# Two modulation groups moved from the delta stage into the ring of weight slabs and the norm chains

## The chip, the core and the metric

The kernel runs on one core of a Trainium2 chip. The metric is the device time of one execution in microseconds. Engines are named as in the profile: PE is TensorE, DVE VectorE, ACT ScalarE, POOL GpSimd, and SP is the engine whose queue issues most of the transfers.

## The reference, cut to what matters

A two-layer encoder step works on 256 prompt tokens and 64 decode tokens, D = 1024. Layer 0 is a gated delta-rule mixer with a dense SwiGLU, layer 1 is forgetting attention with an eight-expert mixture. Each sub-layer is scaled, shifted and gated by vectors made from a condition `c`:

```python
mod = (sc @ p['ada_w'][l] + p['ada_b'][l])[:, None, :]
sh_m, sc_m, gt_m, sh_f, sc_f, gt_f = jnp.split(mod, 6, axis=-1)
h = _rmsnorm(x, p['pre_mix_g'][l]) * (1 + sc_m) + sh_m
...
x = x + gt_m * _rmsnorm(y, p['post_mix_g'][l])
...
kvm = (sc @ p['kv_ada_w'] + p['kv_ada_b'])[:, None, :]
sh_kv, sc_kv = jnp.split(kvm, 2, axis=-1)
```

`sc` is silu(c) for the two streams, so these products have two rows, while their weights are 2 x 24 MB and 8 MB in float32: 56 slabs of 1 MB.

## The kernel before

**Modulation.** The 56 slabs form seven groups of eight: groups 0 to 2 are layer 0, group 3 the shared key/value modulation, groups 4 to 6 layer 1. `ada_load` puts slab n into a ring of six places of its own. `ada_pe` is called with a count of units: a unit is either the four products of one slab (L323, which add into bank 0), or, as the ninth unit of a group, the turn (L330). Before the turn ACT copies the bank to `ada_rows` (L339), and after it DVE adds the bias into `mod` (L350). Group 0 is done in the setup stage; groups 1 to 6 are done in `unit_phase` and `delta_phase`, from calls of `ada_pe`, `ada_act` and `ada_dve` written between the stage's own steps by hand. The calls of the three engines have to name the same units in the same order.

**Delta stage.** The loop over `steps` has 15 steps, five levels for each of three items (two of 8 heads, one of 4). A step is `update(j)` (L1346, L1349), one unit, `product(j + 2)` (L1332), one more unit. DVE masks each product (L1586) and ACT copies each update back (L1716, L1721). After the loop come `off` (L1356), `join` (L1364), the state products (L1369 and others) with further units between them, then a norm, whose output feeds `w_out`. The scratch of this stage lies in the memory of the weight ring, so that `w_out` slabs load only from its end on.

**Weight ring.** All other weights pass as slabs of 1 MB through `raw`, six places. `load(n)` waits on SP until slab n - 6 is split (`raw_split`), then issues one transfer, or two of half a slab for `ffn_up`. ACT and DVE split a slab into a high and a low part (L268, L275) two slabs ahead of PE (`AHEAD`), and `dense_tiles` does the products, three for each pair of parts (L354 to L356).

**Mixed phase.** `mixed_phase` runs twice here: `w_out` (4 slabs), and `ffn_down` (12 slabs). Its last part is the norm chain: PE sums squares over the partitions (L768, L770, then L772, L774), ACT makes the inverse root, DVE adds the residual and forms the next norm (L862 to L866), and ACT ends it (L816, L817). On SP the phase issues the loads six slabs ahead; the first of the two then also stores the last rows of the convolution, and waits for those stores:

```python
for n in range(n0, n0 + n_slabs):
    k.load(sp, n + RAW)
if row_out is not None:
    sp.wait_ge(sig["copied"].sem, copied0 + QKV_T // 4)
    for q in range(QKV_T // 4):
        ...
        k.store(sp, 0, k.o["conv"][s][0, 0][:, 512 * q:512 * q + 512], row_out[rows, q // 4, :])
    sp.wait_ge(k.stores[0], k.n_store[0])
```

**Blocks.** Each phase is one `nc.Block()` with a program for each engine. At its end all engines wait for each other; in the trace these are the rows "PEq L735" and the like.

After the first mixed phase comes `ffn_up_phase` (22 slabs), after the second `copy_phase` with `kv_w` (4 slabs). Both begin with the rest of the norm (`Renewal.act`, `Renewal.dve`), and their tiles wait for it.

Of the kernel before, what the change touches and what calls it, by code (L numbers as in the profile page):

```python
# [54 lines left out]
ADA_GROUP = 8  # L55

# [108 lines left out]
def ada_slabs(i):  # L165

    def wide(w, c0, c1):
        w = w.rearrange("(k p) n -> p k n", p=P)
        return [w[:, k0:k0 + KT // 2, c:c + 512] for c in range(c0, c1, 512) for k0 in (0, KT // 2)]
    ada = i["ada_w"]  # L170
    return wide(ada[0], 0, 6 * D) + wide(i["kv_ada_w"], 0, 2 * D) + wide(ada[1], 0, 6 * D)


class Kernel:


    def __init__(self, nc, ctx, i, o):
# [4 lines left out]
        self.ada_src = ada_slabs(i)  # L182
        sb = self.sb
# [33 lines left out]
        self.junk = self.x_flat[:, KT * T + T:KT * T + T + 1]  # L217
# [27 lines left out]
    def load(self, sp, n):  # L245

        if n >= len(self.slabs):
            return
        if n >= RAW:
            sp.wait_ge(self.raw_split, n - RAW + 1)  # L250
        for words, cols, kts, src in self.slabs[n]:
            width = sum(part[1] for part in self.slabs[n])
            sp.dma_start(self.slab_view(self.raw, n % RAW, words, cols, kts, width), src).then_inc(self.raw_full[n % RAW], 16)

    def full_count(self, n):

        return 16 * sum(len(self.slabs[m]) for m in range(n % RAW, n + 1, RAW))
# [4 lines left out]
    def split_hi(self, act, n):  # L262

        words = self.used(n)
        act.wait_ge(self.raw_full[n % RAW], self.full_count(n))
        if n >= SPL:
            act.wait_ge(self.split_read, n - SPL + 1)
        act.activation(self.w_hi[:, n % SPL, 0:words], self.raw[:, n % RAW, 0:words], ACT.Copy).then_inc(self.hi_ready, 1)  # L268

    def split_lo(self, dve, n):  # L270

        words = self.used(n)
        dve.wait_ge(self.raw_full[n % RAW], self.full_count(n))
        dve.wait_ge(self.hi_ready, n + 1)
        dve.tensor_tensor(self.w_lo[:, n % SPL, 0:words], self.raw[:, n % RAW, 0:words],  # L275
                          self.w_hi[:, n % SPL, 0:words], ALU.subtract).then_inc(self.raw_split, 1)
# [14 lines left out]
    def ada_load(self, sp, n):  # L291
# [3 lines left out]
        sp.dma_start(self.ada_ring[n % (2 * SPL)], self.ada_src[n]).then_inc(self.ada_full[n % (2 * SPL)], 16)  # L295

# [16 lines left out]
    def ada_pe(self, pe, count=1):  # L313


        for g, j, n in self.ada_unit("pe", count):
            if j < ADA_GROUP:
                pe.wait_ge(self.ada_full[n % (2 * SPL)], 16 * (n // (2 * SPL) + 1))
# [3 lines left out]
                for q in range(KT // 2):  # L322
                    last = pe.matmul(self.ps[0][32 * q:32 * q + 32, :],  # L323
                                     self.c_pad[:, half * (KT // 2) + q, C_AT - 2 * block:C_AT - 2 * block + 32],
                                     self.ada_ring[n % (2 * SPL)][:, q, :], start=(j == 0), stop=(j == ADA_GROUP - 1))
                last.then_inc(self.ada_read, 1)
            else:
                pe.wait_ge(self.ada_copied, g + 1)
                for q in range(4):
                    last = pe.matmul(self.ps[0][:, 8 * q:8 * q + 8], self.ada_rows[:, q * P:(q + 1) * P], self.ada_sum[:],  # L330
# [3 lines left out]
    def ada_act(self, act, count=1):  # L334

        for g, j, n in self.ada_unit("act", count):
            if j == ADA_GROUP:
                act.wait_ge(self.ada_read, n)
                act.activation(self.ada_rows[:], self.ps[0][:], ACT.Copy).then_inc(self.ada_copied, 1)  # L339

    def ada_dve(self, dve, count=1):

        for g, j, n in self.ada_unit("dve", count):
            if j == ADA_GROUP:
                dve.wait_ge(self.ada_turned, g + 1)
                tiles = slice(16 * g, 16 * g + 16)
                mod = self.mod[:, tiles, :].rearrange("p (j q) s -> p q j s", q=4)
                bias = self.vec_a[:, tiles].rearrange("p (j q) -> p q j", q=4).unsqueeze(3).to_broadcast([P, 4, 4, 2])
                got = self.ps[0][:, 0:32].rearrange("p (q j s) -> p q j s", q=4, j=4)
# [31 lines left out]
def setup_phase(k):  # L381
# [3 lines left out]
    with nc.sbuf_tensor("row_squares", [P, D], F32) as row_squares, \  # L385
# [59 lines left out]
        def _(sp):  # L445
            for n in range(ADA_GROUP - 1):
                k.ada_load(sp, n)
            k.load(sp, 0)
            k.ada_load(sp, ADA_GROUP - 1)
            for n in range(1, 3):  # L450
                k.load(sp, n)
# [268 lines left out]
def mixed_phase(k, n0, n_slabs, n_k, x_hi, x_lo, gate, gain, sums, renewal, row_out=None):  # L720
# [14 lines left out]
    with nc.Block() as block:  # L735
# [20 lines left out]
        def _(pe):  # L756
# [8 lines left out]

            dense_tiles(k, pe, n0, n_slabs, n_k, x_hi, x_lo, k.ps[0:6], bank_free, half_done=sig["part"].sem, last_slab=old_sums)
            pe.wait_ge(sig["summed"].sem, summed0 + KT - 2)
# [136 lines left out]

def conv_phase(k, h32, h_hi, h_lo, qkv, z_silu, last_rows, lnb, g):
# [6 lines left out]
    with nc.sbuf_tensor("xp", [P, 4, T + 6], F32) as xp, nc.sbuf_tensor("conv_acc", [P, 2, T + 3], F32) as acc, \  # L912
# [11 lines left out]
        def _(sp):  # L924
            for n in range(n0 + 3, n0 + n_slabs):
# [3 lines left out]
                k.load(sp, n)  # L929
# [187 lines left out]
def delta_phase(k, qkv, lnb, g, oT, z_silu, hi, lo, last_rows):  # L1117
# [19 lines left out]
    with ExitStack() as mem:  # L1137
# [101 lines left out]
        def _(sp):  # L1239
            sp.dma_start(state[1][:], i["state_delta"][0, 0].rearrange("h a e -> a h e")).then_inc(state_in, 16)  # L1240
            for n in range(ADA_GROUP + 2 * SPL, 7 * ADA_GROUP):
                k.ada_load(sp, n)
            sp.wait_ge(join_done, 2)
            for n in range(3):
                k.load(sp, n_out + n)
            sp.wait_ge(join_done, 4)
            sp.wait_ge(xy_ready, len(steps))
            k.load(sp, n_out + 3)
# [6 lines left out]
        def _(pe):  # L1255
# [146 lines left out]
            for j in range(len(steps)):  # L1402
# [7 lines left out]
                k.ada_pe(pe, 1)  # L1410
# [64 lines left out]
        def _(dve):  # L1475
# [105 lines left out]
            for j, (n, u) in enumerate(steps):  # L1581
# [6 lines left out]
                k.ada_dve(dve, 1)  # L1588
# [71 lines left out]
        def _(act):  # L1660
# [51 lines left out]
            for j, (n, u) in enumerate(steps):  # L1712
# [11 lines left out]
                k.ada_act(act, 1)  # L1724
# [29 lines left out]
            act.wait_ge(k.ada_read, 7 * ADA_GROUP)  # L1754
# [21 lines left out]
def copy_phase(k, n0, n_slabs, n_k, x_hi, x_lo, dst, scale=1.0, renewal=None, rows=None, caches=None):  # L1776
# [5 lines left out]
    with nc.Block() as block:  # L1782
        @block.sync
        def _(sp):
            if caches is not None:
                caches.sp(sp)
            for n in range(n0, n0 + n_slabs):
                k.load(sp, n + RAW)
# [4 lines left out]
        def _(pe):  # L1793
            def bank_free(tile):
                if tile >= 6:
# [3 lines left out]
                        None if rows is None else lambda n: rows.pe(pe, n))  # L1799

        @block.scalar
        def _(act):
# [8 lines left out]
            for s in range(n_slabs):  # L1811
                if s >= 1 and s % len(n_k) == 0:
                    finish(s // len(n_k) - 1)
                k.ahead_hi(act, n0 + s + AHEAD)
            finish(groups - 1)
# [8 lines left out]
        def _(dve):  # L1824
            if renewal is not None:
                renewal.dve(dve)
            for s in range(n_slabs):
                k.ahead_lo(dve, n0 + s + AHEAD)
                if rows is not None and s < 3:
# [4 lines left out]
def ffn_up_phase(k, h_hi, h_lo, a_hi, a_lo, renewal):  # L1834

    nc, n0, n_slabs = k.nc, k.first["ffn_up"], FT
    with nc.sbuf_tensor("gate_silu", [P, 2, T], F32) as gs, nc.sbuf_tensor("ffn_a", [P, T], F32) as a_own, \
            nc.semaphore("gate_ready") as gate_ready, nc.semaphore("a_ready") as a_ready, \
            nc.semaphore("a_hi_ready") as hi_ready, nc.semaphore("a_lo_ready") as lo_ready, nc.Block() as block:
        a32 = (a_own[:], k.y_flat[:, KT * T:KT * T + T])  # L1840
        @block.sync
        def _(sp):
            for n in range(n0, n0 + n_slabs):
                k.load(sp, n + RAW)

        @block.tensor
        def _(pe):
# [3 lines left out]
            dense_tiles(k, pe, n0, n_slabs, [KT], h_hi, h_lo, k.ps[0:6], bank_free, lambda kt: renewal.ready(pe, kt))  # L1851

        @block.scalar
        def _(act):
# [12 lines left out]
            for s in range(n_slabs):  # L1867
                if s >= 1:
                    silu(s - 1)
                k.ahead_hi(act, n0 + s + AHEAD)  # L1870
                if s >= 1:
# [5 lines left out]
        def _(dve):  # L1877
# [13 lines left out]
            for s in range(n_slabs):  # L1891
                if s >= 1:
                    product(s - 1)
                k.ahead_lo(dve, n0 + s + AHEAD)
                if s >= 1:
# [5 lines left out]
def value_phase(k, h_hi, h_lo, h32, v_new, logf, past_logf, f_cols, neg_rows, past_k, k_past_t, caches_in, query):  # L1901
# [4 lines left out]
    with nc.sbuf_tensor("lf_t", [P, 3, FH], F32) as lt, \  # L1906
# [17 lines left out]
        def _(sp):  # L1924
            for n in range(n0, n0 + n_slabs):
                k.load(sp, n + RAW)
# [400 lines left out]
def moe_phase(k, mem, renewal, h32, h_tok, row, w, idx_f, idx, rounds, slots, scattered_in, y_in, final, gates_ready):  # L2327
# [19 lines left out]
    with ExitStack() as sems:  # L2347
# [122 lines left out]
        def _(sp):  # L2470
# [5 lines left out]
            for g in range(RAW, ROUND_SLABS):  # L2476
                k.load(sp, n0 + g)
# [7 lines left out]
            def again(r):  # L2485
                for g in range(ROUND_SLABS):
                    e, j = divmod(g, EXPERT_SLABS)
                    slot_n = (n0 + g) % RAW
# [148 lines left out]
        def _(act):  # L2637
# [23 lines left out]
            def split(r, g):  # L2661
                m = n0 + g
                act.wait_ge(k.raw_full[m % RAW], full_count(r, g))
                act.wait_ge(k.split_read, r * ROUND_SLABS + (m - SPL + 1))
                act.activation(k.w_hi[:, m % SPL, :], k.raw[:, m % RAW, :], ACT.Copy).then_inc(k.hi_ready, 1)  # L2665
# [75 lines left out]
        def _(dve):  # L2741
# [67 lines left out]
            def split(r, g):  # L2809
                m = n0 + g  # L2810
                dve.wait_ge(k.raw_full[m % RAW], full_count(r, g))
                dve.wait_ge(k.hi_ready, r * ROUND_SLABS + (m + 1))
                dve.tensor_tensor(k.w_lo[:, m % SPL, :], k.raw[:, m % RAW, :], k.w_hi[:, m % SPL, :],  # L2813
# [163 lines left out]
def build(nc, i, o):  # L2977
    ctx = ExitStack()
    with ctx:
# [3 lines left out]
        ada_mem = ctx.enter_context(ExitStack())  # L2983
        k.c_pad = ada_mem.enter_context(nc.sbuf_tensor("c_pad", [P, KT, 32 + C_AT], F32))
        k.ada_rows = ada_mem.enter_context(nc.sbuf_tensor("ada_rows", [P, 512], F32))
        k.ada_sum = ada_mem.enter_context(nc.sbuf_tensor("ada_sum", [P, 8], F32))
        k.vec_a = ada_mem.enter_context(nc.sbuf_tensor("vec_a", [P, 112], F32))
# [20 lines left out]
        with ExitStack() as gdn:  # L3008
# [11 lines left out]
            with nc.sbuf_tensor("lnb", [P, GC], F32) as lnb, nc.sbuf_tensor("g", [P, GC], F32) as g:  # L3020
# [7 lines left out]
                k.ada_units(range(1, 7))  # L3028
# [71 lines left out]
```

## Time and profile before

| | |
|---|---|
| runs | 1710.0, 1710.21 and 1708.83 us, median 1710.0 |
| profiled execution | span 1707.3 us from first to last instruction; its time with what lies around is not listed apart |
| median less span | 2.7 us |
| PE | 1597.9 us busy, 94% |
| PE weight loads | 1338.4 us, 78% |
| DVE, ACT | 1162.7 us (68%), 958.6 us (56%) |
| delta stage with its entry | about 168 to 350.5 us |
| first mixed phase | 350.6 to 394.6 us |
| second mixed phase, its end | 645.7 us |

PE's matmul rows overlap each other and their ends are modelled, so that the distance from one start to the next is the better measure of a product. "SPq" rows are issues or waits of the SP queue.

### The profile page before, as it was taken

Reading aid. Unit: us, or ns where it says so; the run is one execution under the profiler, and the core shown is the slowest. Engines: PE = TensorE matmul, PEld = TensorE weight load, DVE = VectorE, ACT = ScalarE, POOL = GpSimd, SP = SyncE. Lnnn points to the kernel's source line nnn. Section 1 sums busy time; section 2 is a strip of 40 time slices with the busy share of each in tenths; the row PEclk is TensorE's granted clock in tenths of the full one; section 3 lists DMA queues with packets and bytes.
Section 4 is the critical chain, followed back from the end, with each engine's and each line's share of the span. In section 5 each row is a group of like instructions: output and inputs, shape, how many; then the busy total and the mean of one; then the engine's idle time right before and its main releaser. Section 6 shows DMA issues by size and latency. Waiting matters only on the chain. (4 is left out here: it accounts for less than half of the span.)

```text
span 1707.3 us, 25672 instructions
## 1 busy us (share of the span) xinstructions
PE 1597.9 (94%) x10492; PEld 1338.4 (78%) x10492; DVE 1162.7 (68%) x1234; ACT 958.6 (56%) x1170; POOL 101.6 (6%) x193
## 2 busy tenths in 40 slices
PE   6999889987999997997789999999999999999997
PEld 3999466776999997994567888888888888888884
DVE  3875621377444455436684888888888888888887
ACT  2553422375333444324665777777777777777775
POOL 2210100000000000000001000010101010000020
PEclk8999999998999998998898999999999999999999
DMA  9720989764553444349135999999999999999995
GB/s 322 236 75 3 369 308 382 252 160 123 148 149 112 160 124 149 100 154 352 39 110 184 358 359 380 368 378 372 370 383 360 385 356 383 368 378 353 375 378 183
DMA packets 267672, 447.93 MB, mean 262 GB/s; under 512 B 12693, under 2 KB 125550, under 8 KB 267538
## 3 DMA queue, kind: packets, MB, share of 16 engines
q1 hardware_dynamic: 263192, 431.59, 72.6%
q0 software_dynamic: 3632, 13.11, 2.0%
q8 instruction: 85, 1.39, 0.3%
q10 hardware_dynamic: 720, 1.50, 0.3%
q14 instruction: 43, 0.34, 0.1%
HBM read 421.68 MB, written 24.48 MB: 261 GB/s over the span
## 5 line engine op out<-in xcount | busy, mean ns | idle before, releaser
L2813 DVE TENSOR_TENSOR w_lo_late<-raw,w_hi_late 128x2048 fp32r<-128x2048 f32 x262 | 597.8, 2290 | 102.8 <-ACT w_hi_late L2665 101.1
L2665 ACT ACTIVATE w_hi_late<-raw 128x2048 fp32r<-128x2048 f32 x262 | 502.1, 1917 | 156.4 <-PE bank L356 155.1
L354 PE MATMUL bank<-w_hi_late,hg_hi 128*128 128x512 f32 (+1 forms) x768 | 291.8, 380 | 0.8 <-DVE w_lo_late L2813 0.8
L356 PE MATMUL bank<-w_hi_late,hg_lo 128*128 128x512 f32 (+1 forms) x768 | 289.8, 377 | 0.0
L355 PE MATMUL bank<-w_lo_late,hg_hi 128*128 128x512 f32 (+1 forms) x768 | 288.1, 375 | 0.0
L275 DVE TENSOR_TENSOR w_lo_main<-raw,w_hi_main 128x2048 fp32r<-128x2048 f32 (+1 forms) x50 | 112.5, 2249 | 86.6 <-ACT w_hi_main L268 86.6
L356 PEld LDWEIGHTS bank<-w_hi_late,hg_lo 128*128 128x128 f32 x768 | 144.5, 188 | 29.1
L355 PEld LDWEIGHTS bank<-w_lo_late,hg_hi 128*128 128x128 f32 x768 | 144.3, 188 | 28.8
L354 PEld LDWEIGHTS bank<-w_hi_late,hg_hi 128*128 128x128 f32 x768 | 144.2, 188 | 28.9 <-DVE w_lo_late L2813 1.2
L354 PE MATMUL bank<-w_hi_late,act_hi 128*128 128x512 f32 x352 | 141.4, 402 | 0.8 <-DVE w_lo_late L2813 0.7
L356 PE MATMUL bank<-w_hi_late,act_lo 128*128 128x512 f32 x352 | 139.9, 397 | 0.0
L355 PE MATMUL bank<-w_lo_late,act_hi 128*128 128x512 f32 x352 | 138.7, 394 | 0.0
L354 PE MATMUL bank<-h_ffn_hi,w_hi_main 128*128 128x320 f32 x352 | 110.2, 313 | 8.3 <-DVE h_ffn_lo L665 8.3
L268 ACT ACTIVATE w_hi_main<-raw 128x2048 fp32r<-128x2048 f32 (+1 forms) x50 | 94.5, 1889 | 30.6 <-PE bank L356 30.3
L355 PE MATMUL bank<-h_ffn_lo,w_hi_main 128*128 128x320 f32 x352 | 109.7, 312 | 0.0
L356 PE MATMUL bank<-h_ffn_hi,w_lo_main 128*128 128x320 f32 x352 | 109.7, 312 | 0.0
L354 PE MATMUL bank<-h_mix_hi,w_hi_in 128*128 128x320 f32 x256 | 83.5, 326 | 4.1 <-DVE h_mix_lo L1032 3.0
L355 PE MATMUL bank<-h_mix_lo,w_hi_in 128*128 128x320 f32 x256 | 79.9, 312 | 0.0
L356 PE MATMUL bank<-h_mix_hi,w_lo_in 128*128 128x320 f32 x256 | 79.9, 312 | 0.0
L354 PEld LDWEIGHTS bank<-w_hi_late,act_hi 128*128 128x128 f32 x352 | 66.1, 188 | 16.4 <-issue 2.1
L356 PEld LDWEIGHTS bank<-w_hi_late,act_lo 128*128 128x128 f32 x352 | 66.1, 188 | 15.7
L355 PEld LDWEIGHTS bank<-w_lo_late,act_hi 128*128 128x128 f32 x352 | 66.2, 188 | 15.2
(536 smaller groups left out, 2806.6 us busy)
## 6 DMA issues: line engine op xcount, KB each, us to landing
raw<-in_moe_w_gate SPq DMA_DIRECT2D x88, 1024.0 KB, 6.9
raw<-in_moe_w_up SPq DMA_DIRECT2D x88, 1024.0 KB, 7.1
raw<-in_moe_w_down SPq DMA_DIRECT2D x88, 1024.0 KB, 6.8
ada_delta<-in_ada_w SPq DMA_DIRECT2D x40, 1024.0 KB, 9.1
raw<-in_gdn_w_in SPq DMA_DIRECT2D x16, 1024.0 KB, 10.3
slot_rows_far<-zero_row SPq DMA_DIRECT2D x1, 12288.0 KB, 40.1
raw<-in_ffn_w_gate SPq DMA_DIRECT2D x22, 512.0 KB, 4.1
raw<-in_ffn_w_up SPq DMA_DIRECT2D x22, 512.0 KB, 5.4
```

The lines of the kernel that those rows point to most:

```text
L268: act.activation(self.w_hi[:, n % SPL, 0:words], self.raw[:, n % RAW, 0:words], ACT.Copy).then_inc(self.hi_ready, 1)
L275: dve.tensor_tensor(self.w_lo[:, n % SPL, 0:words], self.raw[:, n % RAW, 0:words], self.w_hi[:, n % SPL, 0:words], ALU.subtract).then_inc( ...
L354: pe.matmul(out, w_hi, x_hi, start=start, stop=False)
L355: pe.matmul(out, w_hi, x_lo, start=False, stop=False)
L356: return pe.matmul(out, w_lo, x_hi, start=False, stop=stop)
L2665: act.activation(k.w_hi[:, m % SPL, :], k.raw[:, m % RAW, :], ACT.Copy).then_inc(k.hi_ready, 1)
L2813: dve.tensor_tensor(k.w_lo[:, m % SPL, :], k.raw[:, m % RAW, :], k.w_hi[:, m % SPL, :], ALU.subtract).then_inc(k.raw_split, 1)
```

## The change

`ADA_ORDER` puts the groups in the order 0, 1, 2, 5, 6, 3, 4. The first five (`ADA_EARLY`) are done as before, in setup and in the delta stage, and a step of the delta loop now has one unit instead of two. The last two, 3 and 4, leave the stage. Their slabs pass through the weight ring: `ring_order` puts eight behind the second slab of `ffn_up` and eight behind the second of `kv_w`. A place in the ring that such a slab held is free once its product has run (`ada_read`). The products run in the norm chains of the two mixed phases, three behind the last tile, one behind the sum of squares, four at the end, in banks 4 and 7. The turn runs in the second slab of the phase that follows. SP now loads through ring place `at(last) + 6 + 10` in both mixed phases, before the stores. `c_pad` stays allocated, and some small buffers share memory with others.

```diff
+ADA_ORDER = (0, 1, 2, 5, 6, 3, 4)
+ADA_EARLY = 5
...
+def ring_order(first, n_slabs):
+
+    before = {first["ffn_up"] + AHEAD: ADA_EARLY, first["kv_w"] + AHEAD: ADA_EARLY + 1}
+    order = []
+    for n in range(n_slabs):
+        if n in before:
+            order += [("ada", ADA_GROUP * before[n] + j) for j in range(ADA_GROUP)]
+        order.append(("w", n))
+    return order
...
+    def load_next(self, sp):
+
+        p = self.loaded
+        if p >= RAW:
+            kind, n = self.ring[p - RAW]
+            sp.wait_ge(self.raw_split if kind == "w" else self.ada_read, n + 1)
+        kind, n = self.ring[p]
+        full = self.raw_full[p % RAW]
+        if kind == "ada":
+            sp.dma_start(self.ada_tile(n), self.ada_src[n]).then_inc(full, 16)
+        else:
+            for words, cols, kts, src in self.slabs[n]:
+                width = sum(part[1] for part in self.slabs[n])
+                sp.dma_start(self.slab_view(self.raw, p % RAW, words, cols, kts, width), src).then_inc(full, 16)
+        self.loaded += 1
...
+    def ada_banks(self, g):
+
+        return (self.ps[0], self.ps[0]) if g < ADA_EARLY else (self.ps[4], self.ps[7])
...
             if row_out is not None:
                 sp.wait_ge(k.stores[0], k.n_store[0])
-                k.load(sp, n0 + 4)
-                k.load(sp, n0 + 5)
-            for n in range(n0, n0 + n_slabs):
-                k.load(sp, n + RAW)
+            k.load_through(sp, k.at(n0 + n_slabs - 1) + RAW + (AHEAD + ADA_GROUP if modulation else 0))
             if row_out is not None:
                 sp.wait_ge(sig["copied"].sem, copied0 + QKV_T // 4)
                 for q in range(QKV_T // 4):
...
             dense_tiles(k, pe, n0, n_slabs, n_k, x_hi, x_lo, k.ps[0:6], bank_free, half_done=sig["part"].sem, last_slab=old_sums)
+            if modulation:
+                pe.wait_ge(emptied, emptied0 + 2 * 6)
+            modulate(3)
             pe.wait_ge(sig["summed"].sem, summed0 + KT - 2)
...
+            modulate(1)
             pe.wait_ge(sig["crossed"].sem, crossed0 + KT)
...
+            modulate(4)
...
+def modulated(k, pe):
+
+    def after(s, step):
+        if s == 1 and step == 2 * KT - 1:
+            k.ada_pe(pe, 1)
+    return after
...
-            for n in range(ADA_GROUP + 2 * SPL, 7 * ADA_GROUP):
+            for n in range(ADA_GROUP + 2 * SPL, ADA_EARLY * ADA_GROUP):
...
                     off(0)
-                k.ada_pe(pe, 1)
             off(1)
             k.ada_pe(pe, 1)
...
+                if s == 0:
+                    k.ada_act(act, ADA_GROUP + 1)
...
+                if s == 2:
+                    k.ada_dve(dve, ADA_GROUP + 1)
```

## Rows read from the trace of the kernel before

**Rows 1.** The page's 40 slices of the span, PE busy and GB/s.
```profile
PE   6999889987999997997789999999999999999997
...
GB/s 322 236 75 3 369 308 382 252 160 123 148 149 112 160 124 149 100 154 352 39 110 184 358 359 380 368 378 372 370 383 360 385 356 383 368 378 353 375 378 183
```

**Rows 2.** A stretch of the delta loop, all engines: start:end, length, busy, PE clock, DMA share, GB/s.
```profile
260.00:280.00 20.00, 19.50 (x420) 12.12 (x416) 1.81 (x3) 3.94 (x9) 0.00 (x0) 1.00 1.05 382
```

**Rows 3.** The SP queue's waits in the delta stage, whole run.
```profile
SPq L295 <- PE bank L323: 106.2, 38, 13.1
```

**Rows 4.** PE in order of time, one part of the loop: start, us, what.
```profile
290.93 1.15 PE L1332 MATMUL bank<-raw 64*64 64x64 f32 x32
292.01 1.07 PE L323 MATMUL bank<-ada_delta,c_pad 128*32 128x512 f32 x8
293.00 1.15 PE L1346 MATMUL bank<-raw 64*64 64x64 f32 x32
...
295.02 1.06 PE L323 MATMUL bank<-ada_delta,c_pad 128*32 128x512 f32 x8
```

**Rows 5.** All engines in order of time, norm chain of the first mixed phase.
```profile
383.32 2.29 DVE L275 TENSOR_TENSOR w_lo_main<-raw,w_hi_main 128x2048 fp32r<-128x2048 f32 x1
...
386.06 0.81 PE L768 MATMUL bank<-squares,ones 128*128 128x320 f32 x2 [3.30 <-DVE squares L828]
...
388.32 1.43 PE L772 MATMUL bank<-mix_sums,ones 128*128 128x320 f32 x2 [0.78 <-DVE mix_sums L835]
...
394.75 0.82 DVE L617 TENSOR_TENSOR yT<-xT 128x640 f32<-128x640 f32 x1 [1.40 <-PEq L735]
```

**Rows 6.** The SP queue's own waits, 340 to 400 us: in total, times, longest.
```profile
SPq L735 <- PEq L735: 12.4, 1, 12.4
...
SPq L735 <- DMA out_conv<-row_out: 2.6, 1, 2.6
```

**Rows 7.** PE's groups by line, 168 to 345 us: the turns and their waits.
```profile
L330 PE MATMUL bank<-ada_sum,ada_rows 128*128 128x8 f32 x48 | 6.1, 254 | 3.7 <-ACT ada_rows L339 3.7
```

**Rows 8.** The costliest groups by form, 130 to 360 us, a DVE row.
```profile
L1586 DVE TENSOR_TENSOR raw<-bank,masks 128x512 f32<-128x512 f32 x10 | 6.9, 688 | 30.2 <-PE bank L1332 30.2
```

**Rows 9.** PE in order of time, from the loop's last step on.
```profile
305.26 3.57 PE L323 MATMUL bank<-ada_delta,c_pad 128*32 128x512 f32 x16
...
317.69 1.92 PE L323 MATMUL bank<-ada_delta,c_pad 128*32 128x512 f32 x16
...
321.53 1.06 PE L323 MATMUL bank<-ada_delta,c_pad 128*32 128x512 f32 x8
...
327.99 0.96 PE L330 MATMUL bank<-ada_sum,ada_rows 128*128 128x8 f32 x8
```

**Rows 10.** Stretches in which `w_out` slabs and then `ffn_up` slabs load.
```profile
318.00:326.00 8.00, 8.00 (x71) 5.75 (x64) 1.29 (x2) 3.28 (x4) 0.00 (x0) 1.00 1.10 348
...
353.00:367.00 14.00, 14.00 (x96) 14.00 (x95) 10.06 (x15) 3.69 (x7) 0.00 (x0) 1.00 1.16 292
```

**Rows 11.** The modulation slabs by tile: issue to landing.
```profile
DMA to landing us min/median/max: 5.2/9.0/15.7
```

**Rows 12.** The SP queue in order of time, delta stage and first mixed phase.
```profile
168.86 7.33 SPq L295 DMA_DIRECT2D ada_delta<-in_ada_w  x6
...
350.66 0.38 SPq L253 DMA_DIRECT2D raw<-in_ffn_w_gate  x1
...
359.00 1.74 SPq L253 DMA_DIRECT2D raw<-in_ffn_w_gate  x1
...
375.34 4.19 SPq L359 DMA_DIRECT2D out_conv<-row_out  x12
```

**Rows 13.** The same for the second mixed phase.
```profile
634.02 2.29 DVE L275 TENSOR_TENSOR w_lo_main<-raw,w_hi_main 128x2048 fp32r<-128x2048 f32 x1 [4.74 <-ACT w_hi_main L268]
...
637.57 0.70 PE L768 MATMUL bank<-squares,ones 128*128 128x320 f32 x2
...
645.79 0.37 SPq L2306 DMA_DIRECT2D past_k<-in_cache_k  x1
```

More of the change, by code:

```diff
@@ L170, in ada_slabs @@
     ada = i["ada_w"]
-    return wide(ada[0], 0, 6 * D) + wide(i["kv_ada_w"], 0, 2 * D) + wide(ada[1], 0, 6 * D)
+    every = wide(ada[0], 0, 6 * D) + wide(i["kv_ada_w"], 0, 2 * D) + wide(ada[1], 0, 6 * D)
+    return [every[ADA_GROUP * g + j] for g in ADA_ORDER for j in range(ADA_GROUP)]
+def ring_order(first, n_slabs):
[6 more added lines that the diff above has]
+    return order
 class Kernel:
@@ L182, in __init__ @@
         self.ada_src = ada_slabs(i)
+        self.ring, self.loaded = ring_order(self.first, len(self.slabs)), 0
+        self.place = {item: p for p, item in enumerate(self.ring)}
         sb = self.sb
@@ L243, in slab_view, with at, slot, parts_at @@
         return t[:, slot, 0:kts * width].rearrange("p (k n) -> p k n", k=kts)[:, :, words:words + cols]
[L245 to L253, printed above, removed]
+    def at(self, n):
+        return self.place["w", n]
+    def slot(self, n):
+        return self.at(n) % RAW
+    def parts_at(self, p):
+        kind, n = self.ring[p]
+        return len(self.slabs[n]) if kind == "w" else 1
+    def load_next(self, sp):
[3 more added lines that the diff above has]
+            sp.wait_ge(self.raw_split if kind == "w" else self.ada_read, n + 1)
+        kind, n = self.ring[p]
+        full = self.raw_full[p % RAW]
[6 more added lines that the diff above has]
+        self.loaded += 1
+    def load_through(self, sp, p):
+        while self.loaded <= min(p, len(self.ring) - 1):
+            self.load_next(sp)
+    def full_at(self, p):
+        return 16 * sum(self.parts_at(q) for q in range(p % RAW, p + 1, RAW))
     def full_count(self, n):
-        return 16 * sum(len(self.slabs[m]) for m in range(n % RAW, n + 1, RAW))
+        return self.full_at(self.at(n))
     def used(self, n):
@@ L329, in ada_pe @@
                 for q in range(4):
[L330 removed]
+                    last = pe.matmul(self.ada_banks(g)[1][:, 8 * q:8 * q + 8], self.ada_rows[:, q * P:(q + 1) * P], self.ada_sum[:],
                                      start=True, stop=True)
@@ L447, in _ @@
                 k.ada_load(sp, n)
-            k.load(sp, 0)
+            k.load_through(sp, 0)
             k.ada_load(sp, ADA_GROUP - 1)
-            for n in range(1, 3):
-                k.load(sp, n)
+            k.load_through(sp, 2)
         @block.gpsimd
@@ L1773, in _, with copy_phase @@
                 high(n)
-def copy_phase(k, n0, n_slabs, n_k, x_hi, x_lo, dst, scale=1.0, renewal=None, rows=None, caches=None):
+def copy_phase(k, n0, n_slabs, n_k, x_hi, x_lo, dst, scale=1.0, renewal=None, rows=None, caches=None, modulation=False):
     nc = k.nc
@@ L1786, in _ @@
                 caches.sp(sp)
-            for n in range(n0, n0 + n_slabs):
-                k.load(sp, n + RAW)
+            k.load_through(sp, k.at(n0 + n_slabs - 1) + RAW)
             if rows is not None:
@@ L1798, in _ @@
                         None if renewal is None else lambda kt: renewal.ready(pe, kt),
-                        None if rows is None else lambda n: rows.pe(pe, n))
+                        None if rows is None else lambda n: rows.pe(pe, n),
+                        modulated(k, pe) if modulation else None)
         @block.scalar
@@ L1814, in _ @@
                 k.ahead_hi(act, n0 + s + AHEAD)
+                if s == 0 and modulation:
+                    k.ada_act(act, ADA_GROUP + 1)
             finish(groups - 1)
@@ L1828, in _ @@
                 k.ahead_lo(dve, n0 + s + AHEAD)
+                if s == 2 and modulation:
+                    k.ada_dve(dve, ADA_GROUP + 1)
                 if rows is not None and s < 3:
@@ L1924, in _ @@
         def _(sp):
-            for n in range(n0, n0 + n_slabs):
-                k.load(sp, n + RAW)
+            k.load_through(sp, k.at(n0 + n_slabs - 1) + RAW)
             sp.wait_ge(ready, 1)
```

94 lines of the change are left out of this document (53 added, 41 removed).

## The prediction

> **What bounds the kernel now.** I read the page's 40 slices first [rows 1]. PE is near full nearly everywhere, so the time is mostly the sum of PE's work and of a few holes. The reader is to see two kinds of stretch. From slice 4 to 7 the DMA moves up to 382 GB/s: that is the delta stage, which streams 48 modulation slabs. From slice 8 to about 17 it moves 100 to 160 GB/s beside a full PE, so there the transfers have room. The windows of the delta loop show both at their limit: PE 19.50 of 20 us busy, DMA share 1.05 [rows 2]. SP waits there 38 times for PE to read a slab, 106.2 us in all [rows 3], and PE's waits for slabs are few, so PE's own order sets the pace and a product taken out is worth its PE time. The order of time on PE gives that: a slab's product starts at 292.01 and the next work at 293.00, so 1.0 us for a unit [rows 4].
>
> Then I read the two norm chains, where the products go, in order of time. In the first, PE stands idle 3.30 us before the sum of squares at 386.06 and again before 388.32, and DVE opens the next block at 394.75 [rows 5]. SP had been done long before: it waits 12.4 us at the end of the block [rows 6]. That wait is the cover under which anything new on SP would be free, and this change uses it up.
>
> **Part 1, delta stage.** Removed are 16 products and two turns, 18 units. Fifteen calls leave the loop. Up to the end of the last update 14 units go, 14 x 1.0 = 14.0 us. The waits before a turn stay alike: the turns of all six groups cost 3.7 us of waiting for ACT's copy [rows 7], and the two that are left in the loop stand behind an update, where that wait is longest; I count 0.4 us less waiting. That is -14.4 us. What is left in a step of 8 heads is 1.1 us of product, 2.0 us of update and 1.0 us of one unit on PE, against one masking of 0.69 us on DVE [rows 4, 8], and the result of each is wanted only a step later; so PE goes on setting the pace.
>
> Behind the loop, two products with a wait for a slab between them (3.57 us) become one without (1.0): -2.5. Then `off`, `join` and three products are as before. The pair at 317.69 becomes one turn, but it had hidden ACT's copies of `v_tok`, for which the next products wait, so of the 0.9 us I count nothing, and +0.1 for ACT's copy for the last turn, which now stands ahead of the copies of `inv`. The product at 321.53 goes, -1.0, and the turn at 327.99 goes, -1.0, since it is done earlier [rows 9]. Sum -4.4. The delta stage: -18.8 us. Bounds: -12, if half of the loop's 14.0 us went to waits that the units now cover, and -21, if the pair at 317.69 gave its 1.9 us too.
>
> **Part 2, the two turns moved.** Each is eight matmul records of about 1.0 us in a stretch where PE is full, so +2.0 us. A slab is 2 x 8 x 3 = 48 products, and 96 of them fill 14 us, so 7.0 us [rows 10]; ACT's and DVE's parts, under 0.7 us each by DVE's row for a bank of 512 columns [rows 8], lie beside it; if they did not, +2.8 us.
>
> **Part 3, end of the first mixed phase.** This decides. SP now has to issue, ahead of the twelve stores: `ffn_up` 0 and 1, eight modulation slabs, and `ffn_up` 2 to 7. Modulation slab 4 takes the place of `ffn_up` 0, slab 5 that of `ffn_up` 1, which DVE has split at 383.32 + 2.29 = 385.61 [rows 5]. Slabs 6 and 7 wait for the products of 0 and 1, and `ffn_up` 2 to 7 for those of slabs 2 to 7. The first three products fit PE's idle 3.30 us, so all of these waits are over soon, but none before 382.8. So from 385.61 on nine slabs have to move in one queue: three modulation slabs and six of `ffn_up`.
>
> Their pace: a lone modulation slab lands 5.2 us from its issue [rows 11], a further one in 1.05 MB / 382 GB/s = 2.7 us [rows 2], and an `ffn_up` slab in 1.05 / 292 = 3.6 us [rows 10]. Slab 5 lands at 390.8, 7 at 396.2, `ffn_up` 7 at 396.2 + 6 x 3.6 = 417.8. Does SP have to stay for this? The issues say yes: a half slab of `ffn_up` issues in 0.38 us when the queue is empty and in 1.74 when it is full, which is its transfer time, and six modulation slabs took 7.33 us, where 0.4 each would be 2.4 [rows 12]. So SP is held until at most two halves of `ffn_up` are left: the last issue returns at about 417.8 - 3.6 = 414.2. The twelve stores take 4.19 us to issue [rows 12] and another 2.6 us until they have landed [rows 6]: 414.2 + 4.2 + 2.6 = 421.0, or, if they only wait behind the loads, 417.8 + 2.6 = 420.4; I take 420.5. With 0.2 us for the block's end DVE's first `times`, and with it every tile of `ffn_up`, starts at 420.7 and not at 394.75: +26.0 us. The norm chain and PE's last product (397.2) are over by then. Bounds: +10.3, if SP were never held (last product 397.2, last load issued 398.2, stores issued 402.4 and landed 405.0), and +30, if the nine slabs go 4 us slower than the rows of single kinds.
>
> The Trainium skill (DMA: Bandwidth & Descriptors, Queues, rings and completion order) says that descriptors are consumed in ring order, and that a semaphore's increment lands only behind the earlier writes of its DMA engine. By that rule the stores can't be counted as landed before `ffn_up` 7 at 417.8, and the sum would hardly change. The rows of before, where the stores met one slab ahead of them, don't tell it apart.
>
> **Part 4, end of the second mixed phase.** There are no stores. Slab 5 waits for the split that ends at 634.02 + 2.29 = 636.3 and lands at 641.5, slab 7 at 646.9. The three products come just when the sum of squares could run, at 637.57 [rows 13], and push the chain at most 3.0 us back; PE's last product ends at 647.9. But SP has `kv_w` 2 and 3 and four slabs of the next weight to issue behind slab 7. They have the form of `w_out`'s, 348 GB/s or 3.0 us [rows 10], and two of them may be outstanding: six modulation slabs in 7.33 us are four at 0.4 and two at 2.7 us [rows 12], so four slabs in pieces of 2 KB fit in the queue, or two halves of `ffn_up` in pieces of 0.5 KB, and so two slabs in pieces of 1 KB. The last issue returns at 646.9 + 4 x 3.0 = 658.9. With 0.4 us for the block's end the next phase starts at 659.3 instead of 645.79 [rows 13]: +13.5 us. Bounds: +3.0 (SP not held, the chain decides) and +16.5 (one slab outstanding).
>
> **Everything else.** The steady part of `ffn_up` and of `kv_w` needs one slab in 7.0 us and gets one in 3.6 or less; the backlog hides there. The renamed ring places, the reordered groups and the shared buffers cost nothing, since the group is there one phase before its use.
>
> **The sum.** -18.8 + 2.0 + 26.0 + 13.5 = +22.7 us. On the span: 1707.3 + 22.7 = 1730.0. The median of the runs lies 2.7 us over the span, so 1732.7: I say 1733.
>
> **Rivals.**
> - *The gain survives (the other side).* SP is not held by a full queue and the stores pass the loads: -18.8 + 2.0 + 10.3 + 3.0 = -3.5, or 1706 us. It decides from the point where the two block ends together slip by less than 16.8 us. For it speak the issues of 0.38 us wherever the queue is empty, and against it 1.74 and 7.33 us where it is full [rows 12]. Chance 0.10. The Trainium skill (the same page, Issuing engines are not separate DMA queues) calls the sequencer's time to initiate a DMA usually small beside the DMA itself; by that rule this rival would come true but for the stores. The trace disagrees for a full queue.
> - *One end only.* SP is held by the wait for its stores, but issues alone don't hold it at the second end: -18.8 + 2.0 + 26.0 + 3.0 = +12.2, 1722 us. Chance 0.10.
> - *The delta stage gives less.* DVE's and ACT's chain, not PE, takes over in the loop: -9 instead of -18.8, 1743 us. Against it: a masking of 0.69 us has a step of about 4 us as cover [rows 4, 8]. Chance 0.08.
> - The change does what it says in any case, since the slabs and products do move. My forecast has 0.72.
>
> **How the numbers follow.** The forecast's own range comes from the delta stage's bounds and some 4 us either way on the queue: 1725 to 1740. For 8 in 10 I leave out the first rival and half of the third: 1718 to 1742. A difference under 0.2% (3.4 us) can't be told from none here. Slower: forecast, second and third rival less a little, 0.82. The first rival lies at the edge: faster 0.11, same 0.07.
>
> **What the profile after would show.** In the loop one L323 group of eight records for each update, and the stage about 19 us shorter. In the first mixed phase modulation slabs issued near 385.6 (less the delta gain), then half slabs of `ffn_up` at 1.7 us an issue, the twelve stores last, SP the last to reach the block's end, and DVE, ACT and PE waiting there for some 24 us. In the second, SP last again, PE idle some 11 us more. If SP's wait at the end of both blocks is still long, the prediction is wrong.

## The result and the profile after

The kernel after takes 1739.99 us in the median (1731.66 to 1741.53, four runs), the kernel before 1710.11 us in the same comparison. The ratio is 1.0163 [1.0147, 1.0179]: 29.9 us, or 1.6%, slower. The forecast was 1733 us in a range of 1718 to 1742. The profiled execution took 1738.82 us, its span 1737.0, which is 29.7 more than the span before.

To see where this came from I cut the spans of the two profiled executions at the ends of the program's blocks, which every engine passes together.

| stage | before, us | after, us | difference | forecast |
|---|---|---|---|---|
| unit phase, to its end | 186.3 | 187.6 | +1.3 | 0 |
| delta stage | 164.2 | 146.6 | -17.6 | -18.8 |
| first mixed phase | 44.1 | 69.8 | +25.7 | +26.0 |
| `ffn_up` | 164.8 | 166.5 | +1.7 | +1.0 |
| second mixed phase | 86.3 | 96.8 | +10.5 | +13.5 |
| `kv_w` | 37.3 | 38.3 | +1.0 | +1.0 |
| the rest up to the expert stage | 203.4 | 202.6 | -0.8 | 0 |
| expert stage | 820.9 | 828.8 | +8.0 | 0 |

(The differences are taken before rounding.) The two ends of the mixed phases take more than the delta stage gives, as forecast, and the expert stage adds 8.0 us, which no step of the prediction speaks of.

Some of these stages as windows of the profile after, and last the first mixed phase of the profile before: start:end, length, then busy time of PE, PE's weight loads, DVE, ACT and POOL, then PE's granted clock, the DMA share and GB/s.

```profile
168.60:187.60 19.00, 15.18 (x60) 5.45 (x60) 12.68 (x20) 13.36 (x21) 0.00 (x0) 0.90 0.91 331
187.60:334.20 146.60, 133.68 (x2104) 99.84 (x2104) 55.60 (x122) 47.94 (x90) 6.65 (x10) 0.94 0.66 227
334.20:404.00 69.80, 42.28 (x266) 34.13 (x266) 35.18 (x56) 25.61 (x57) 0.00 (x0) 0.79 0.84 242
...
570.50:667.30 96.80, 88.25 (x602) 80.84 (x602) 45.62 (x57) 39.48 (x65) 0.00 (x0) 0.97 0.63 206
...
908.20:1737.00 828.80, 806.97 (x3746) 649.49 (x3746) 690.79 (x454) 582.03 (x432) 57.66 (x47) 0.98 0.96 346
```
```profile
350.50:394.60 44.10, 33.47 (x202) 30.70 (x202) 35.16 (x56) 25.45 (x57) 0.00 (x0) 0.92 0.56 145
```

The delta stage streams 227 GB/s on average and is no longer at a limit of the DMA. The first mixed phase has 42.28 us of PE work in 69.80 us. What holds it shows in the SP queue in order of time (start, us from the first issue's start to the last one's end, line, what, how often):

```profile
334.34 0.38 SPq L288 DMA_DIRECT2D raw<-in_ffn_w_gate  x1
...
337.96 33.58 SPq L284 DMA_DIRECT2D raw<-in_kv_ada_w  x8
372.03 0.37 SPq L288 DMA_DIRECT2D raw<-in_ffn_w_gate  x1
372.44 4.11 SPq L288 DMA_DIRECT2D raw<-in_ffn_w_up  x1
...
381.70 1.74 SPq L288 DMA_DIRECT2D raw<-in_ffn_w_gate  x1
...
394.38 1.74 SPq L288 DMA_DIRECT2D raw<-in_ffn_w_up  x1
396.16 5.13 SPq L422 DMA_DIRECT2D out_conv<-row_out  x12
```

Of the 33.58 us of the modulation slabs 28.5 are waits for places in the ring (27.4 for splits, 1.1 for products). The twelve halves of `ffn_up` 2 to 7 leave SP between 372.03 and 396.12, one behind the other, at 1.7 us each once the queue is full. Only then do the twelve stores leave; the last of their issues returns at 401.29. SP's waits at the end of the block answer to [rows 6]:

```profile
SPq L797 <- DMA out_conv<-row_out: 2.3, 1, 2.3
SPq L797 <- PEq L797: 0.2, 1, 0.2
```

SP had waited 12.4 us for PE there; now the others wait for SP. The first instruction of the next block shows for how long, in order of time, all engines, in both phases (the number in brackets is the idle time ahead):

```profile
404.07 0.83 DVE L679 TENSOR_TENSOR yT<-xT 128x640 f32<-128x640 f32 x1 [25.58 <-PEq L797]
...
405.00 0.93 ACT L665 ACTIVATE yT<-yT,mod,coef_next 128x256 f32<-128x256 f32 x2 [25.41 <-DVE yT L679]
...
667.40 2.57 SPq L2386 DMA_DIRECT2D past_k<-in_cache_k  x1
667.46 0.82 DVE L679 TENSOR_TENSOR yT<-xT 128x640 f32<-128x640 f32 x1 [9.45 <-PEq L797]
```

The same instruction had 1.40 us of idle time in [rows 5]. The name behind the arrow (PEq) is that of the block end's handshake and not the late one: PE was done at 381.2. Two windows of the wait say who works in it:

```profile
381.40:404.00 22.60, 0.00 (x0) 0.00 (x0) 0.00 (x0) 0.00 (x0) 0.00 (x0) 0.51 1.04 253
659.10:667.30 8.20, 0.00 (x0) 0.00 (x0) 0.00 (x0) 0.01 (x1) 0.00 (x0) 0.66 1.10 348
```

No engine computes anything for 22.6 and 8.2 us, while the DMA is full with weights that nobody needs yet.

In the expert stage the difference sits in one place, behind ACT's last copy in the program's first round:

```profile
1711.95 0.60 ACT L2778 ACTIVATE slot_out<-bank 128x512 f32<-128x512 f32 x1 [6.03 <-PE bank L419]
1725.56 1.06 ACT L3003 ACTIVATE raw<-xT 128x1024 f32<-128x1024 f32 x1 [13.01 <-issue]
```

Between these two, ACT waits for nothing that the profile shows. In the profile before, the same pair is 5.37 us apart and the second waits for DVE's `xT`:

```profile
1689.47 0.60 ACT L2698 ACTIVATE slot_out<-bank 128x512 f32<-128x512 f32 x1 [6.02 <-PE bank L356]
1694.84 1.06 ACT L2923 ACTIVATE raw<-xT 128x1024 f32<-128x1024 f32 x1 [4.77 <-DVE xT L2941]
```

### The profile page after: what moved, and what is told of

Read it like the earlier page. It is cut to its first block and busy times, and to the rows that moved or that the text cites. A ratio compares the mean times of both kernels' runs of the same rounds, so it can differ in the third digit from the quotient of the medians.

```text
span 1737.0 us, 25672 instructions
## 1 busy us (share of the span) xinstructions
PE 1599.4 (92%) x10492; PEld 1345.3 (77%) x10492; DVE 1164.3 (67%) x1234; ACT 959.5 (55%) x1170; POOL 101.3 (6%) x193
## 5 line engine op out<-in xcount | busy, mean ns | idle before, releaser
L417 PEld LDWEIGHTS bank<-h_ffn_hi,w_hi_main 128*128 128x128 f32 x352 | 67.3, 191 | 28.9 <-issue 26.9
## 6 DMA issues: line engine op xcount, KB each, us to landing
raw<-in_gdn_w_in SPq DMA_DIRECT2D x16, 1024.0 KB, 11.1
```

Of the source, the lines that this page charges most:

```text
L417: pe.matmul(out, w_hi, x_hi, start=start, stop=False)
```

## The experiments

Two questions were open. Is it the position of SP's loads that costs the two ends, and if so the issuing itself or the stores that follow it? And where do 8 us in the expert stage come from, where both kernels do the same work?

**Loads later.** In both mixed phases SP loads only up to the eighth modulation slab; the slabs behind it are issued at the start of the next phase.

```diff
-            k.load_through(sp, k.at(n0 + n_slabs - 1) + RAW + (AHEAD + ADA_GROUP if modulation else 0))
+            k.load_through(sp, k.at(n0 + n_slabs - 1) + (AHEAD + ADA_GROUP if modulation else RAW))
```

> The changed kernel, but SP's loads in both mixed phases stop behind the eighth modulation slab; the six weight slabs behind it are issued at the start of the next phase. Nothing is left out. Theory A (the full queue ahead of the block's end holds SP): in the first mixed phase SP is done near the landing of the last modulation slab and the stores (about 385 us by the changed kernel's clock instead of 403.8), so that phase is 51 us long instead of 69.8; the second is 91 us instead of 96.8 because PE's last product ends at 659 and not SP at 667; both next phases grow by less than 2 us. Sum -24 us: 1713 to 1718. Theory B (the products in the norm chain delay the block's end): both phases keep their length, 1738 to 1742.

Measured: 1712.0 us (1708.71 to 1713.34, ten runs), 1.0008 [0.9994, 1.0021] of before and 28.0 us less than after. The first mixed phase takes 48.0 us instead of 69.8, the second 90.4 instead of 96.8: 28.2 us together. The phases that now issue these loads did not grow (165.7 and 37.8 us). So the position of these loads explains all that the ends lost, but for 3.9 and 4.1 us that stay. The SP queue in order of time and its wait for the stores:

```profile
337.86 32.52 SPq L284 DMA_DIRECT2D raw<-in_kv_ada_w  x8
370.42 3.99 SPq L422 DMA_DIRECT2D out_conv<-row_out  x12
381.87 0.41 SPq L288 DMA_DIRECT2D raw<-in_ffn_w_gate  x1
```
```profile
SPq L797 <- DMA out_conv<-row_out: 7.0, 1, 7.0
```

The stores were issued by 374.41 and landed 7.0 us later, where 2.3 us do when little is ahead of them. The modulation slabs, issued by 370.38, were still in the queue: PE waited for the last of them until 379.44. The kernel still gains nothing over the kernel before: the expert stage takes 831.0 us, and ACT's idle time without a cause is there with 15.1 us.

**The delta stage alone.** The two groups that left the delta stage are left out altogether: no loads, products or turns of them, and their modulation vectors are zero, so that what is computed behind them is another function of the input.

> The delta stage's part alone: groups 3 and 4 are not loaded and not multiplied at all, their vectors are set to zero by one memset, so the outputs behind them are not the reference's. Theory A: the gain of the delta stage stays whole, 16.3 us up to the start of the first mixed phase, the two mixed phases have the length of before (44.1 and 86.3 us), and the time is about 1694 (1690 to 1702 with the stall at the end). Rival: part of the 25.7 and 10.5 us that the mixed phases grew by comes with the new ring or the new banks and not with the slabs; then this kernel stays above 1700 by its mixed phases.

Measured: 1687.57 us (1685.97 to 1688.57, four runs), 0.9872 [0.9847, 0.9896]. The first mixed phase begins at 332.7, 17.8 us earlier than before, and both mixed phases take exactly what they took before, 44.1 and 86.3 us. That undershoots what was expected; the excess lies in the expert stage, 815.7 us, 5.2 less than before. With zero vectors the gate sees other values, and what that does there was not separated. It need not be the cause: up to ACT's last copy of the first round the stage takes 798.1 us here and 803.0 before, but also 798.6 in the next run, which computes everything. For the times the run counts ahead of the expert stage only. ACT's idle time without a cause is not there: the pair of rows is 5.5 us apart, though the source of the expert stage is that of the kernel after; ACT's program is shorter ahead of it.

**Stores first.** In the first mixed phase the twelve stores are issued ahead of the last ten loads, and the wait for them stands behind all.

```diff
-            k.load_through(sp, k.at(n0 + n_slabs - 1) + RAW + (AHEAD + ADA_GROUP if modulation else 0))
+            k.load_through(sp, k.at(n0 + n_slabs - 1) + RAW)
...
+            if modulation:
+                k.load_through(sp, k.at(n0 + n_slabs - 1) + RAW + AHEAD + ADA_GROUP)
+            if row_out is not None:
                 sp.wait_ge(k.stores[0], k.n_store[0])
```

> The changed kernel, with the twelve stores of the first mixed phase issued ahead of the last ten loads, and the wait for them last. Nothing is left out. Theory A1 (SP is held by the issues of the loads as well): the block ends when the last load has been issued, at about 392 to 397 instead of 404.0, so -7 to -12 us. Theory A2 (only the wait for the stores holds SP, issues don't): the block ends with PE's last product at 381.3, so -22 us.

Measured: 1732.72 us (1727.65 to 1735.88, four runs), 1.0141 [1.0113, 1.017]. The SP queue, and the first instructions behind the block's end:

```profile
358.06 3.92 SPq L422 DMA_DIRECT2D out_conv<-row_out  x12
363.31 7.78 SPq L284 DMA_DIRECT2D raw<-in_kv_ada_w  x4
...
394.20 1.74 SPq L288 DMA_DIRECT2D raw<-in_ffn_w_up  x1
396.44 0.83 DVE L679 TENSOR_TENSOR yT<-xT 128x640 f32<-128x640 f32 x1 [18.40 <-PEq L797]
```

There is nothing left for the stores to wait for, and SP has no wait for them in its list; yet the block ends at 396.3, right behind the last issue (394.20 + 1.74 = 395.94). So the issues alone hold the block. The order of the stores is worth 7.4 us in this phase, the issuing and landing of the twelve (5.13 + 2.3); the other 18.3 us of the phase's excess remain.

**ACT padded.** The kernel after with 40 waits on a semaphore that has long been reached, at the start of ACT's part of the expert stage. They become 20 instructions (the trace has 25692 instead of 25672) and wait for nothing; they move the code behind them.

```diff
             renewal.act(act)
+            for n in range(40):
+                act.wait_ge(k.split_read, n + 1)
             act.wait_ge(logits_done, 1)
```

> The changed kernel with 40 waits on ACT that are long satisfied, at the start of the expert phase. Nothing is left out. It is for the 8 us by which the last phase grew, where ACT stands before its last loop's branches with no wait that the profile shows. Theory L (where ACT's instructions lie in memory decides): the gap of 13.0 us before the last phase's first square becomes another one in this kernel's profile, likely the 4.8 us of before, and the time falls by 7 to 8 us. Theory T (it comes and goes with the execution): runs of this kernel and of the changed one both spread over some 10 us.

Measured: 1730.19 us (1729.05 to 1730.53, four runs), 1.0119 [1.0095, 1.0144] of before, 9.8 us less than after: work was added, and the time fell. The expert stage takes 821.2 us, 7.6 less than in the kernel after; the rest of the 9.8 lies elsewhere, 2.1 us of it ahead of the first mixed phase. The chain of waits of the kernel after, in the place of the idle time (start, us, what; ACTq is ACT's sequencer at the branches of the loop over further rounds, none of which are run here):

```profile
1712.10 0.06 ACTq L2481
1712.16 2.45 issue
1714.61 0.05 ACTq L2480
1714.66 2.41 issue
1717.07 0.06 ACTq L2480
1717.12 3.17 issue
...
1720.41 2.99 issue
...
1723.44 2.03 issue
```

And that of the padded kernel, where the chain goes over DVE instead:

```profile
1710.86 0.07 DVEq L2481
1710.93 2.80 issue
1713.73 0.05 DVEq L2480
...
1713.89 0.28 issue
```

ACT had stood for 2.0 to 3.2 us at each of five steps between branches, 13.05 us in all. Now one step of 2.80 us on DVE is left, which the kernel before has too. The expectation had 7 to 8 us, which is what the expert stage gave.

**Loads later, and padded.** The first and the fourth edit together.

> e1_loads_later with the 40 satisfied waits on ACT of e4_act_padded. Nothing is left out. Theory L (the place of ACT's last loop in its code costs 8 to 10 us at the end) says that the last phase is 821 us long as before and the time 1702 (1700 to 1705), 0.4% under before. Theory T (chance of an execution) says 1709 to 1712 as e1_loads_later.

Measured: 1703.37 us (1702.33 to 1709.31, twelve runs), 0.9965 [0.9952, 0.9978]: faster than before. The phases take 48.1 and 90.4 us, the expert stage 823.3 (821 expected). The padding gives 8.6 us here, against 9.8 in the fourth; in the expert stage alone it is 7.7 against 7.6.

**Fewer products in the chain.** The fifth kernel, with two of the eight products of the first mixed phase moved to the start of `ffn_up`, and four of the second to the start of `kv_w`; those left in the second run at the end of its chain.

```diff
-            modulate(3)
+            modulate(3 if row_out is not None else 0)
...
-            modulate(1)
+            modulate(1 if row_out is not None else 0)
...
-            modulate(4)
+            modulate(2 if row_out is not None else 4)
...
+            if modulation:
+                k.ada_pe(pe, 4)
...
+            k.ada_pe(pe, 2)
```

> e5_later_padded with the products placed otherwise: in the first mixed phase 3, 1 and 2 and the last two at the start of ffn_up; in the second none until the chain's last sum, then 4, and 4 at the start of kv_w. Nothing is left out. In e1_loads_later the two phases are 3.9 and 4.1 us longer than before; if this is PE's last products and the pushed sum of squares, they become 44 to 45 and 86 to 87 us, the next phases grow by up to 1 us each, and the time is 1696 (1694 to 1700). If it is the transfers themselves, it stays at 1702.

Measured: 1699.14 us (1697.23 to 1703.22, six runs), 0.9933 [0.9914, 0.9952], the fastest of the kernels that compute everything, though its interval touches the fifth's. The second mixed phase falls from 90.4 to 87.9 us, where 86 to 87 were expected, so the products in the chain did cost it 2.5 of its 4.1 us. The first stays at 48.0 and misses the 44 to 45 expected: PE is done at 374.2 and ACT at 376.4, but SP comes at 380.1. Its SP queue:

```profile
368.88 3.97 SPq L422 DMA_DIRECT2D out_conv<-row_out  x12
380.31 0.41 SPq L288 DMA_DIRECT2D raw<-in_ffn_w_gate  x1
```

SP waits 7.0 us for the stores behind 372.85, as in the first run. So in the first phase it is the stores behind the modulation slabs that decide here, not the products. With all eight products in the chain the two lay close together: in the first run PE's last product ended at 380.5 and the stores landed at 381.4.

**The kernel before, one instruction more.** The kernel before with one wait more at the end of ACT's loop body over further rounds. That body is never run, and the rest is untouched.

```diff
-            more_rounds(act, n_rounds, run_round)
+            def run_and_one_more(r):
+                run_round(r)
+                act.wait_ge(k.hi_ready, 1)
+            more_rounds(act, n_rounds, run_and_one_more)
```

> The kernel before with one more instruction in ACT's program, a wait at the end of the body of the loop over further rounds; no execution reaches it, since there is one round only. Nothing is left out. The changed kernel's ACT program has one instruction more in that body too. Theory L says that this alone brings the gap of 13 to 15 us before the last phase's first square and 7 to 10 us: 1717 to 1720. Theory T, or a cause in the moved products, says 1709 as before. If the boundary is not crossed by exactly this instruction, the result is open.

Measured: 1718.22 us (1714.5 to 1722.1, nine runs), 1.0049 [1.0033, 1.0065]: 8.3 us slower than before through an instruction that is never run. The gap appears, in order of time on ACT:

```profile
1693.82 0.60 ACT L2698 ACTIVATE slot_out<-bank 128x512 f32<-128x512 f32 x1 [6.14 <-PE bank L356]
1708.51 1.06 ACT L2926 ACTIVATE raw<-xT 128x1024 f32<-128x1024 f32 x1 [14.09 <-issue]
```

The expert stage takes 829.0 us, 8.1 more than before, as in the kernel after (8.0). So nothing that the change does on SP, PE or the DMA is needed for this cost. That in the kernel after it comes from one instruction more in the same body of ACT's program was expected and isn't shown: the body is never run, so that no trace holds it. The kernel with the delta stage alone has the same source there and no gap, so that instruction by itself doesn't bring it about; where the code lies does.

## Why the prediction was right

**What bounds the kernel, part 1.** "PE's own order sets the pace and a product taken out is worth its PE time" held. The loop took 75.4 us before and 62.1 after, 13.3 us less for a forecast of 14.4, and what lies behind it gave 4.8 for 4.4. The third rival, by which DVE and ACT take over in the loop and the stage gives 9 us, is refuted by the 17.6 that it gave. In the loop there is one group of eight records per update, as foretold:

```profile
284.25 1.15 PE L1407 MATMUL bank<-raw 64*64 64x64 f32 x32
285.23 1.10 PE L1421 MATMUL bank<-raw 64*64 64x64 f32 x32
286.17 1.10 PE L1424 MATMUL bank<-raw 64*64 64x64 f32 x32
287.20 1.07 PE L386 MATMUL bank<-ada_delta,c_pad 128*32 128x512 f32 x8
```

SP's waits for PE fell with it; to [rows 3] answers the first of these rows, and to [rows 2] the window below it:

```profile
SPq L340 <- PE bank L386: 82.0, 19, 14.7
```
```profile
260.00:280.00 20.00, 17.55 (x420) 14.57 (x418) 3.02 (x6) 4.40 (x9) 0.00 (x0) 0.91 0.67 224
```

The mixed phase began 16.3 us earlier and not 18.8. Of the difference, 1.3 us lie ahead of the delta stage, where PE ran its 60 matmuls in 15.18 us at a mean clock of 0.90 instead of in 13.69 at 1.00. The change on PE is not the cause of that: the padded kernel has the same code on PE and ran that stretch at 1.00, and its mixed phase began at 332.1, 18.4 us earlier than before. The fifth and sixth kernels gave 18.0 and 18.3. Of the seven kernels with the new delta stage, the kernel after, the first run and the third show this fall of the clock; the padded ones and the one with the delta stage alone don't. With one profile of each, chance and the place of the code aren't told apart. So the term was right within 0.8 us, and what is missing even there fits a smaller clock: between 270 and 280 us all kernels with the new delta stage show a clock of 0.83 and about 8.1 to 8.3 us of PE work, where the kernel before shows 1.00 and 9.50.

**Part 2, the turns.** +2.0 forecast; `ffn_up` and `kv_w` together took 2.7 us more, near the upper of the two values that were given (2.8). Which part of it is the turns and which the products' shadows was not separated.

**Part 3, the first end.** +26.0 forecast, +25.7 measured, and by the steps given. Read 16.3 us earlier for the earlier start, modulation slab 7 was to land at 379.9; PE got it at 380.12. PE's last product was to end at 380.9 and ended at 381.2. The last issue was to return at 397.9; it did at 396.12, 1.8 us earlier, and twelve issues of stores then took 5.13 us where 4.19 were put. The stores were to have landed at 404.2 and DVE to start at 404.4; they landed at 403.6, and DVE started at 404.07. That the end is met within 0.3 us is so in part since small misses offset each other. The rival by which SP is not held by a full queue is refuted by the run with the stores first, and the second rival, by which issues alone don't hold it at the second end, by the 8.2 us that the other engines wait there for SP without a store. The Trainium skill (DMA: Bandwidth & Descriptors, Issuing engines are not separate DMA queues) calls the time to initiate a DMA usually small beside the DMA itself. These runs agree while the queue is empty (0.38 us) and disagree when it is full (1.74 us for a half slab, again and again).

The question that the rows before left open is told apart by the first and the third run: stores behind a backlog of slabs land 7.0 us late, stores behind nothing new land while SP does other things. The Trainium skill (the same page, Queues, rings and completion order) says that on each DMA engine descriptors are consumed in ring order; the 7.0 us agree with it.

**Part 4, the second end.** The mechanism was right, the size too large: +13.5 forecast, +10.5 measured (+12.3 in the padded kernel and +12.4 in the one with the stores first, whose phases began with a stretch on PE that was 1.5 us longer). Read 11.1 us later, slab 7 was to land at 658.0; PE has it at 657.92. What failed is the step by which "two slabs in pieces of 1 KB" may be outstanding. From that landing to the return of the last issue (664.09 + 2.92 = 667.01) pass 9.1 us, three slabs of 3.0 and not four, so of the six slabs behind slab 7 three were still in the queue. In the padded kernel it is 9.1 us as well.

**Everything else** was put at nothing, and that was wrong by 8.0 us, which is why the median is 7 us over the forecast. The cost hangs on where ACT's code lies, shown from both sides: taken away with 20 idle instructions (-9.8 and -8.6 us, of them 7.6 and 7.7 in the expert stage), brought about with one that is never run (+8.3 us). Over all nine profiles the two rows of ACT are 13.6 to 15.7 us apart in the four kernels with the gap and 5.4 to 5.5 in the five without. The stage as a whole varies by some 5 us more for reasons not found: with the gap it takes 825.4 to 831.0 us, without it 820.9 to 823.3 (815.7 with zero vectors). That ACT there waits for its own instructions to be brought isn't shown, but the DMA queue that the page of the profile calls "instruction" fits it. It lists (packets, MB, share) 47 packets for each of the four kernels with the gap, 43 for the kernel before and the one with the delta stage alone, and 41 for the padded ones. The difference lies in the gap itself. Between 1712 and 1725.6 us of the kernel after, with at least one packet in each of the five steps:

```profile
q14 instruction: 11, 0.09, 2.3%
```

and in the same place of the kernel before, between 1689.5 and 1694.9:

```profile
q14 instruction: 4, 0.03, 1.9%
```

Whether these packets are ACT's isn't told by the trace.

**The sum.** Up to the expert stage the kernel was to lose 22.7 us and lost 21.8, but partly by luck, since two errors cancel: the mixed phase began only 16.3 us earlier, 2.5 less than forecast, and the second end cost 3.0 less. With the unforeseen 8.0 us the median stands 2 us under the upper end of the range; without the error at the second end it would have lain outside. The side on which the change came out didn't hang on either, nor on the expert stage: without the 8 us it would still be some 1.2% slower, as the padded kernel was.

**What stays open:** which addresses or distances in ACT's program make the branches slow, and why PE's clock falls for a few microseconds ahead of the delta stage in three of the nine profiles and not in the others.

## What to carry to other kernels

Work moved off a full engine is only half of the change: follow what the queue that feeds it must now issue ahead of the next point where all engines meet, and count an issue at the transfer time of its data as soon as the queue is full. Loads that only the next phase needs belong behind that point; here that alone gave back 28 us. Stores that are waited for belong ahead of a backlog, which was worth 7.4 us. When a difference is left in a stage with the same work, read the idle time that nothing explains, and move the code by a few idle instructions before seeking the cause in the data.

## What the hardware showed beyond that

- One instruction more in a loop body of ACT that is never run cost 8.3 us in the kernel before, 0.49% [0.33, 0.65], in steps of 2.1 to 3.3 us at the branches around it. A change of a kernel's source can thus gain or lose 8 us in a stage whose work it leaves alone.
- An engine that issues into a full queue is held for as long as the data ahead takes: each half slab of `ffn_up` held SP for 1.74 us, where the first of the phase took 0.38.
- With work taken out of PE's sequence its granted clock was lower in places. The stretch from 240 to 250 us shows 0.98 in the kernel before, 0.91 in that kernel with one instruction more, and 0.74 to 0.81 in all seven kernels with the new delta stage. After idle times of 1.67 and 0.86 us an update that takes 1.10 us at full clock took 1.97; in the kernel before, the same update took 1.57:

```profile
240.49 1.97 PE L1421 MATMUL bank<-raw 64*64 64x64 f32 x32 [0.86 <-DVE raw L1660]
```
